# Banded attention of a two-block model: score column for the sinks, division on GpSimd, v as features, other step order

## The reference

```python
def sliding_window_attention(q, k, v, sinks):
    # q: 16 heads of 64, k and v: 2 heads of 64; blocks of 128 queries
    # each block reads its own and the previous block of 128 keys
    ...
        bias = jnp.where(valid, alibi, MASK_VALUE)
        s = einsum('bqhgd,bkhd->bhgqk', qi, kb) * scale + bias
        m = jnp.maximum(jnp.max(s, axis=-1, keepdims=True), sink)
        p = jnp.exp(s - m)
        denom = jnp.sum(p, axis=-1, keepdims=True) + jnp.exp(sink - m)
        return einsum('bhgqk,bkhd->bqhgd', p / denom, vb)

def swa_layer(x, norm_g, w_in, q_g, k_g, sinks, w_out):
    proj = rms_norm_2(x, norm_g) @ w_in          # q, k and v
    q, k = rms_norm_2(q, q_g), rms_norm_2(k, k_g)
    return x + sliding_window_attention(q, k, v, sinks) @ w_out
```

## Time and profile before

| | |
|---|---|
| median of the runs | 2334.64 us |
| the profiled execution | 2337.08 us |
| its span | 2335.3 us |
| PE, DVE, ACT, POOL busy | 96%, 41%, 36%, 39% |
| granted clock of PE, mean | 0.97 |
| banded attention, first projection to last output product | 1778.5 to 1971.4 us of the span |

### The profile page before, as it was taken

One profiled execution on the slowest core, in us unless ns is written; L12 is line 12 of the kernel. 1 busy time (PEld: TensorE's weight loads), 2 busy tenths in 40 slices (PEclk: granted clock), 3 DMA queues, 4 the chain that ended last, 5 costly groups with the idle time before them and its releaser, 6 DMA issues.

```text
span 2335.3 us, 29338 instructions
## 1 busy us (share of the span) xinstructions
PE 2234.3 (96%) x10442; PEld 1832.5 (78%) x10442; DVE 952.2 (41%) x1449; ACT 843.8 (36%) x1244; POOL 909.2 (39%) x383
## 2 busy tenths in 40 slices
PE   6999999999999999999998889999999879999999
PEld 5888887788887788888876668888888768888887
DVE  4222222354534532222225665555322884555500
ACT  4233222422333332323333434444322553444421
POOL 3444444332354244444432123444543104444453
PEclk9999999899999999999998879999999889999999
DMA  4333333212243223333331112332333102333332
GB/s 145 102 93 97 101 108 106 63 60 68 82 127 108 63 90 99 90 100 106 101 128 46 37 46 90 93 105 90 108 108 127 37 19 81 99 90 99 99 108 81
DMA packets 58686, 210.26 MB, mean 90 GB/s; under 512 B 6640, under 2 KB 7408, under 8 KB 58224
## 3 DMA queue, kind: packets, MB, share of 16 engines
q1 hardware_dynamic: 56736, 202.07, 28.2%
q10 hardware_dynamic: 1872, 7.10, 0.8%
HBM read 207.05 MB, written 2.10 MB: 90 GB/s over the span
## 4 chain that ended last, share of the span: by engine, by line
PE 74%; issue 13%; POOL 6%; DVE 5%; ACT 1%; POOLq 0%; DVEq 0%; ACTq 0%
PE psum L208 22%; PE psum L209 22%; PE psum L210 22%; POOL w_lo L182 6%; PE psum L226 1%; PE psum L227 1%; PE psum L228 1%; DVE swa_s L2116 1%; PE psum L1197 1%; PE psum L1172 1%; PE psum L756 1%; DVE swa_most L2122 1%; DVE swa_s L2134 1%; PE psum L1555 0%; PE psum L1954 0%
## 5 line engine op out<-in xcount | busy, mean ns | idle before, releaser
L182 POOL TENSOR_TENSOR w_lo<-w_raw,w_hi 128x1024 fp32r<-128x1024 f32 x379 | 909.0, 2405 | 1407.2 <-ACT w_hi L170 1407.2
L208 PE MATMUL psum<-x_hi,w_hi 128*128 128x512 f32 x1808 | 721.1, 399 | 32.4 <-DMA block_ones<-in_squares 15.3
L209 PE MATMUL psum<-x_lo,w_hi 128*128 128x512 f32 x1808 | 714.1, 395 | 0.0
L210 PE MATMUL psum<-x_hi,w_lo 128*128 128x512 f32 x1808 | 713.4, 395 | 0.0
L170 ACT ACTIVATE w_hi<-w_raw 128x1024 fp32r<-128x1024 f32 x379 | 394.4, 1054 | 617.2 <-PE psum L210 578.1
L208 PEld LDWEIGHTS psum<-x_hi,w_hi 128*128 128x128 f32 x1808 | 345.4, 191 | 110.4 <-DMA block_ones<-in_squares 15.3
L210 PEld LDWEIGHTS psum<-x_hi,w_lo 128*128 128x128 f32 x1808 | 345.1, 191 | 74.5
L209 PEld LDWEIGHTS psum<-x_lo,w_hi 128*128 128x128 f32 x1808 | 345.8, 191 | 72.3 <-issue 0.2
L248 DVE SCALAR_TENSOR_TENSOR x<-psum,x 128x512 f32<-128x512 f32 x64 | 44.3, 692 | 389.8 <-PE psum L210 389.8
L208 PE MATMUL psum<-ffn_hidden_hi,w_hi 128*128 128x512 f32 x352 | 136.9, 389 | 0.0
L209 PE MATMUL psum<-ffn_hidden_lo,w_hi 128*128 128x512 f32 x352 | 136.9, 389 | 0.0
(11 more groups left out here) (309 smaller groups left out, 2599.6 us busy)
## 6 DMA issues: line engine op xcount, KB each, us to landing
w_raw<-in_stream SPq DMA_DIRECT2D x379, 512.0 KB, 3.6
swa_bias<-in_swa_bias ACTq DMA_DIRECT2D x1, 2048.0 KB, 10.7
out<-x SPq DMA_DIRECT2D x8, 256.0 KB, 4.7
ab_bias<-in_ab_bias ACTq DMA_DIRECT2D x1, 1792.0 KB, 7.1
x<-in_x_in SPq DMA_DIRECT2D x4, 256.0 KB, 5.1
x<-in_x_in ACTq DMA_DIRECT2D x4, 256.0 KB, 6.8
xattn_mem<-in_mem ACTq DMA_DIRECT2D x1, 1024.0 KB, 4.8
mix_k_turned<-in_gate_w ACTq DMA_DIRECT2D x1, 256.0 KB, 3.6
```

The source lines that it names most:

```text
L182: pool.tensor_tensor(self.w_lo[:, split, :], self.w_raw[:, raw, :], self.w_hi[:, split, :].bitcast(F32), ALU.subtract).then_inc(self.w_lo_ ...
L208: pe.matmul(out, w_hi, hi[:, k0 + j, :], start=first and j == order[0], stop=False)
L209: pe.matmul(out, w_hi, lo[:, k0 + j, :], start=False, stop=False)
L210: mm = pe.matmul(out, w_lo, hi[:, k0 + j, :], start=False, stop=last and j == order[-1])
```

## The change

**Sinks.** The sinks are written as one more column behind the 256 score columns (`END` is 257). The maximum over 257 columns comes out negated from one reduction, and the sum of the exponentials has the sink in it. A short step uses columns 128 to 256.

**Division.** DVE makes only the reciprocal (`share`). POOL multiplies the probabilities, 64 operations in all, in `WindowAttention.pool`, which also holds the weight splits of this stage; the loop of splits is cut in two around it. The exponentials are written to a tile of their own, `p`, with three buffers; the scores `s` have two.

**v as features.** v is a unit like k, projected behind q1, and PE turns it back to tokens in four transposes.

**Order.** turn_p is now one iteration later on PE, copy and upper one iteration later on ACT and on DVE. q2 and q3 are projected around the first scores. The output projection has its first four units begun early: for tiles 0 to 5 of the result (`EARLY`), in banks 2 to 5, `tensor_part` puts 18 products ahead of turn_p(15), 18 ahead of values(15) and 36 behind it; the other 6 products of each of these units follow.

```diff
 class Out:
+    def tensor_part(self, m, tiles):
+        c.products(c.bank(self.banks[m]), self.u0 + m, self.u0 + m, self.hi, self.lo, order=tiles, last=False,
+                   wait_tile=self.wait_tile if m == 0 else None, done=False)
...
 class WindowAttention:
-    UNITS = ["k", "q0", "v", "q1", "q2", "q3", "q4", "q5", "q6", "q7"]
-    EXTRAS = {0: ["q2", "q3"], 1: ["qstat1"], 2: ["q4"], 4: ["q5"], 5: ["qstat2"], 6: ["q6"], 8: ["q7"], 9: ["qstat3"]}
+    UNITS = ["k", "q0", "q1", "v", "q2", "q3", "q4", "q5", "q6", "q7"]
+    STEPS = 4 * TB
+    PROJECTED = {2: [4], 4: [5], 7: [6], 9: [7]}
+    SQUARED = {0: [2], 1: [3], 3: [4], 5: [5], 8: [6], 10: [7]}
+    STATS = {2: 1, 6: 2, 10: 3}
+    EARLY = [0, 1, 2, 3, 4, 5]
+    PARTS = 4
+    END = 2 * P + 1
...
     def tensor(self, pe):
+        for n in range(self.STEPS):
+            if n + 2 < self.STEPS:
+                scores(n + 2)
+            if n >= 1:
+                turn_p(n - 1)
+            for t in self.PROJECTED.get(n, []):
+                project(f"q{t}")
             if n >= 2:
                 values(n - 2)
-            turn_p(n)
+            if n in self.STATS:
+                query_stats(self.STATS[n])
+        last = self.STEPS - 1
+        pe.wait_ge(self.scores_read, 4 * last)
+        self.out.tensor_part(0, self.EARLY)
+        turn_p(last)
+        values(last - 1)
+        self.out.tensor_part(1, self.EARLY)
+        values(last)
+        pe.wait_ge(self.scores_read, 4 * last + 4)
+        self.out.tensor_part(2, self.EARLY)
+        self.out.tensor_part(3, self.EARLY)
+        self.out.tensor(pe, self.PARTS, self.EARLY)
...
     def scalar(self, act):
+        for n in range(self.STEPS):
+            for t in self.PROJECTED.get(n, []):
+                ahead(f"q{t}")
+            if n >= 2:
+                copy_turned(n - 2)
+            if n >= 3:
+                upper(n - 3)
+            if n + 1 < self.STEPS:
+                exps(n + 1)
+            for tile in self.SQUARED.get(n, []):
+                square(tile + 1, self.q[:, tile % 4, :], f"q{tile}")
+            if n in self.STATS:
+                query_roots(self.STATS[n])
...
     def vector(self, dve):
         def maxima(n):
-            chain.own(dve, dve.tensor_reduce(self.most[:], self.s[:, n % 3, :, 0:width], AX.X, ALU.max))
-            chain.own(dve, dve.tensor_tensor(self.most[:], self.most[:], sinks, ALU.max))
-            chain.own(dve, dve.tensor_tensor(self.sink[:, n % 2, :], sinks, self.most[:], ALU.subtract))
-            own(dve, dve.tensor_scalar(self.negated[:, n % 2, :], self.most[:], -1.0, None, ALU.mult),
-                self.max_ready, n + 1)
+            own(dve, dve.tensor_reduce(self.negated[:, n % 2, :], self.s[:, n % 2, :, first:self.END], AX.X, ALU.max,
+                                       negate=True), self.max_ready, n + 1)
+        def share(n):
+            dve.wait_ge(self.exp_done, 4 * n + 4)
+            if n >= 2:
+                dve.wait_ge(self.p_ready, 4 * (n - 1))
+            own(dve, dve.reciprocal(self.shares[:, n % 2, :], self.sums[:, n % 2, :]), self.shares_ready, n + 1)
...
+        for n in range(self.STEPS):
+            if n >= 2:
+                copy_turned(n - 2)
+            if n >= 3:
+                lower(n - 3)
+            if n - 1 in self.STATS:
+                query_rstd(self.STATS[n - 1])
+            if n + 1 < self.STEPS:
+                maxima(n + 1)
+            if n == 0:
+                take("q3", self.q[:, 3, :])
+            share(n)
+            for t in self.PROJECTED.get(n, []):
+                take(f"q{t}", self.q[:, t % 4, :])
...
+    def pool(self, pool):
+        def divide(n):
+            _, first = self.keys(n)
+            pool.wait_ge(self.shares_ready, n + 1)
+            for head in range(4):
+                p = self.p[:, n % 3, head, first:2 * P]
+                pool.tensor_scalar(p, p, self.shares[:, n % 2, head:head + 1], 1.0, ALU.mult, ALU.mult
+                                   ).then_inc(self.p_ready, 1)
+        u = self.unit("q3") + AHEAD + 1
+        for unit in range(self.pool_first(), u):
+            c.lower(pool, unit, unit)
+        for n in range(self.STEPS):
+            for t in self.PROJECTED.get(n, []):
+                c.lower(pool, u, u)
+                u += 1
+            divide(n)
+        for unit in range(u, self.pool_end()):
+            c.lower(pool, unit, unit)
```

239 lines of the change are left out of this document (109 added, 130 removed).

## The result

The changed kernel takes 2346.77 us (median of six runs, 2345.92 to 2349.02) against 2334.59 us for the kernel before (six runs, 2327.68 to 2336.59). The ratio is 1.0058, with a 95% interval of 1.0046 to 1.0070: slower by more than the 0.2% that can be told from no change. The forecast was 2345. The profiled execution of the changed kernel took 2346.5 us, with a span of 2344.7.

The account below looks back on a forecast made before the run. The order of DVE's and ACT's queues was taken to bound the loop, 6.35 us a full step. Terms 2.9 + 4.3 + 3 + 1.2 = 11.4 us on the 2334.6 median gave 2346, stated as 2345; range 2330 to 2359.

Parts of the forecast that it names:

- closed round: Step loop: maxima on DVE, exps, copy, upper on ACT, lower on DVE, next maxima, no overlap; 6.35 us a full step.
- The decoupled rival: Step loop: rounds decouple and the sum of an engine's work decides; 2310 to 2325 us, centre 2318; chance 0.11.
- The test by which the forecast would fail: Step loop: the forecast fails altogether if DVE's lower finds ACT's upper already done.
- The head: Stage start to first scores: v as a unit, q2 ahead of the scores, 1778.5 to 1812.4; PE one unit further on.
- Its three terms: Stage start to first scores: five PE units 27.2 us, norm and statistics work 4.3, one wait for the first bank 1.7.
- The slow clock: PE after idle gaps of 3 to 4.4 us ahead of units q4 to q7, and at first partial products: 3 us.
- the list of additions: Whole stage: three things on top of +2.9 us, namely 4.3 for norm work, 3 for clock, 1.2 for sink copies.
- the forecast's list of starts: Step loop: predicted starts of maxima(1) to (15), from 1815.6 to 1919.7, and share(15) at 1926.3.
- The burst: Output projection: products 0 to 3 end 1.36 us apart, DVE norm work bunches, eighth x_lo at 1983.4: +4.3 us.
- The sink copies: Step loop: eight copies of sinks into score columns, 0.15 us each, 1.2 us; waits for POOL splits estimated +2 more.
- POOL's division: Step loop: four divisions 2.0 to 2.4 us; rival with it as bound, 1.2 each: 2352 to 2362, chance 0.13.
- 2.9 (round, head and last products): Tail: 192 output products after values(13), with turn_p(15) and two values between, end at 1974.3 against 1971.4: +2.9 us.

Follow-up runs that it names:

- the two moves: Changed kernel with lower(n-3) behind maxima(n+1) on VectorE and the query unit ahead of turn_p(n-1) on PE: 2319.53 us, ratio 0.9940.
- The undo runs: Kernel before with the sinks column alone: 2326.19 us, ratio 0.9970; the same with divisions on POOL, old order: 2331.88 us, ratio 0.9993.

## Why the prediction came out

**The direction was right for the reason given.** The prediction's closed round was priced at 6.35 us for a full step; it measured 6.34 and 6.12 at the end of the loop, with DVE idle for 2.02 us ahead of the lowering and ACT's upper part as releaser. Moving the lowering alone brought the steps to 4.35, the sum that it named as DVE's own. The decoupled rival, 2310 to 2325, is what the two moves together gave (2319.5). The test by which the forecast would fail, a lowering that finds upper done, did not come about in the plain steps; it did only behind the reads of q5 and q6 (1854.43 and 1879.37), where the forecast too has DVE waiting for the unit.

**The head** was priced right: first scores 2.0 us sooner in the stage, with PE one unit further on. Its three terms add up to 33.2 us, where the prediction has 33.9 (1778.5 to 1812.4); measured were 33.7 to the first scores. The whole stage begins 2.6 us sooner (1775.95, not 1778.5), which is no part of the change: over the twelve kernels' profiled executions that start lies anywhere from 1770.9 to 1778.9. So maxima(1) came at 1812.7, where the forecast had 1815.6.

**The slow clock was mis-sized.** It stood in the list of additions as 3 us in all (3 to 6 at the units and about 1 at the first partial products, partly hidden). Against the forecast's list of starts, maxima(1) to (3) came 3 us sooner by the clock of the span, then the lead was lost in steps: 1.9 at maxima(4), 2.6 at (6), 1.5 at (9), 1.3 at (11), which are the steps with q4, q5, q6 and q7, and hardly anything between; from 3.2 us ahead to 3.8 behind, in all 7.0. The rows of PE account for it: a unit (6.60, 7.39, 6.44, 6.63 us) and the turn ahead of it (1.87, 1.94, 1.94 for eight transposes, 1.09 for four) took 1.9, 2.8, 1.8 and 1.6 us more than the forecast's 5.45 and the 1.09 or 0.66 that eight or four transposes take at full clock. The last turn_p and values ahead of the output projection, 1.94 and 2.03 us, cost 1.8 more. So the term was about 9 us and not 3. The error was to price only the unit behind the pause, and from one case, when the short pieces of work behind the pauses of 3 to 4 us ran at 1.2 GHz too. One place came out right by luck: in the interval to maximum 8 the sixteen statistics took 3.58 us instead of 1.84, and yet it was 9.2 us long, as forecast (9.3), so something else there was priced too high.

**The burst was mis-sized the other way.** It was worth 4.3 us in the forecast and nothing in the run. The timeline of DVE in the output projection:

```profile
1955.29 0.69 DVE L249 SCALAR_TENSOR_TENSOR x<-psum,x 128x512 f32<-128x512 f32 x1 [8.92 <-PE psum L211]
1957.05 2.31 DVE L262 SCALAR_TENSOR_TENSOR x_lo<-x,columns,x_hi 128x512 fp32r<-128x512 f32 x1 [1.07 <-ACT x_hi L280]
...
1976.91 1.23 DVE L262 SCALAR_TENSOR_TENSOR x_lo<-x,columns,x_hi 128x512 fp32r<-128x512 f32 x1 [0.86 <-ACT x_hi L280]
...
1983.76 0.75 DVE L262 SCALAR_TENSOR_TENSOR x_lo<-x,columns,x_hi 128x512 fp32r<-128x512 f32 x1 [0.86 <-ACT x_hi L280]
```

The first x_lo took 2.31 us, as in the earlier trace rows, the second and the last 0.75, and the five between 1.22 to 1.46. In the burst they follow each other 3.4 us apart and not 4.7. The eighth was ready at 1984.5, about 1 us before PE came to it (21 products of 0.227 us behind 1980.86), and the next stage began at 1980.86 without a pause of PE. The reason stands in POOL's timeline:

```profile
1974.95 2.64 POOL L181 TENSOR_TENSOR w_lo<-w_raw,w_hi 128x1024 fp32r<-128x1024 f32 x1 [0.77 <-ACT w_hi L170]
```

This split ends at 1977.59, and the x_lo that began at 1976.91 ends at 1978.14, 0.55 us later. In the kernel before, the x_lo of the earlier trace rows at 1968.05 ended at 1970.36, again 0.54 after the end of a split (1967.41, 2.41 us long). So x_lo stands still until POOL's split is over, and its 2.31 us was the rest of a split and not a price of its own. In the burst it comes 2.0 us after the split's start, in the kernel before 0.64 after it, and less is left to wait for. The prediction used the same contention for the sink copies and did not see it in this row. Two of its sums here are off by 0.2 us: 43.6, 1.0 and 2.1 from 1927.4 end at 1974.1, not 1974.3, and seven times 4.7 and 2.2 from 1948.5 at 1983.6, not 1983.4. By its own reckoning the output projection was 46.9 us, and it measured 47.7.

**The sink copies** were put at 1.2 us and took 3.0 in the trace: six of the eight 0.17, but two 1.15 and 0.85. The timelines of DVE and of POOL show what held them:

```profile
1844.51 1.15 DVE L2138 COPY swa_s<-columns 128x4 f32<-128x4 f32 x1
...
1870.70 0.85 DVE L2138 COPY swa_s<-columns 128x4 f32<-128x4 f32 x1
```

```profile
1843.28 2.35 POOL L181 TENSOR_TENSOR w_lo<-w_raw,w_hi 128x1024 fp32r<-128x1024 f32 x1 [1.09 <-ACT w_hi L170]
...
1869.17 2.35 POOL L181 TENSOR_TENSOR w_lo<-w_raw,w_hi 128x1024 fp32r<-128x1024 f32 x1 [2.58 <-ACT w_hi L170]
```

Both ended within 0.03 us of the end of a weight split on POOL. The Trainium skill (SBUF — State Buffer, Who interferes with whom) states an exclusive lock for the whole instruction and not a shared rate; the trace agrees, here and at x_lo, with 1.7 us for the two copies against the estimate of 2 in the prediction. Behind each of the two long ones DVE waited over 4 us for a unit (4.11 and 4.23), so they cost nothing there; of the six short ones at most a few tenths stand on the path.

**POOL's division** came in at four for 1.84 us, less than the 2.0 to 2.4 assumed and far from 4.8. PE waited for it 1.1 us in all. Four of 128 elements took 1.41 us. A quarter of each is 0.46 and 0.35 us: 0.84 ns an element and a fixed part of about 0.24 us. The Trainium skill (GPSIMD Engine Reference, Elementwise) gives 1.03 cycles an element, from which the prediction made an estimate of 0.3 us for 256; the trace's slope is about that page's, and the fixed part comes on top. That the division costs next to nothing holds in the changed kernel and fails in the old order.

**The sum.** The stage was forecast 11.4 us longer and became 12.0 longer. The terms were 2.9 (round, head and last products), 4.3 (burst), 3 (clock) and 1.2 (copies). In their place stand about 3 (what is left of the 12.0), 0, about 9 and nearly 0. That the total is right to 1 us is partly luck: two errors cancel, +6 and -5.5. What was right by mechanism is the round. It takes back the 31.6 us of DVE's work and by this account leaves the stage some 3 us longer. That it is 12 us, enough to be told from no change, is the clock, the term that was too small; that share is reckoned from PE's rows, no run changes the clock alone.

The undo runs give the parts of the change their own worth, in us of the stage, from one profiled execution each. The column gains 9.1 (8.9 by the medians). The division on POOL in the old order gives 7.3 of it back (5.7 by the medians). All parts together with the two moves are 15.8 faster than before, 6.6 beyond the column alone. The same parts in the order that the change gave them are 27.8 slower than that. No run takes out v as a unit or the later turn_p by itself; the 6.6 us are of them and the division together.

## What to carry to other kernels

Before crediting work taken off a full engine, walk one iteration through the in-order queues of the engines that hand it results: if A waits for B's late instruction ahead of producing what B needs next, the sum of both engines' work is the pace, and the saving returns as a wait. Put the instruction that takes a late result behind the independent work of its queue, on each engine, and try the moves together, since one alone can hand its gain to the other's wait. Add the slow clock to every pause of TensorE: here 3 to 4 us of idle time cost 1.6 to 2.8 us of the work behind it. And look whether a duration that you take as a price is the same in all rows; one that has several values may have a wait in it.
